# Attention of the two later layers: heads alternating per query block, and value products per query block in 128 columns

## What is computed

```python
for l in range(2):
    h = rmsnorm(x)
    p = h @ w_in[l]                       # latents of queries and keys, a shared rope key, a convolution's input
    q, k, v = ...                         # 8 heads: queries and keys of 64 + 32 rotated columns, values of 64
    sc = q @ k.T                          # per head 512 x 512
    prob = softmax(sc * scale)            # over all 512 keys, no mask
    y_attn = prob @ v                     # per head 512 x 64
    u = silu(layernorm(dwconv(glu(p))))   # depthwise convolution of 31 taps
    x = x + concat(y_attn, u) @ w_o[l]
    x = x + ffn(rmsnorm(x))
```

## Time and profile before

| | |
|---|---|
| runs, median | 2052.92 us |
| profiled execution, its span | 2052.9 us (no time lies around the span) |
| PE, DVE, ACT busy | 1956.8, 1195.2, 958.2 us |
| chain that ended last | PE 88%, DVE 6%, ACT 3% |
| attention loop, first later layer | 887.4 to 988.4 us |
| attention loop, second later layer | 1516 to 1617 us |

### The profile page before, as it was taken

One profiled execution on the slowest core, in us unless ns is written; L12 is line 12 of the kernel. 1 busy time (PEld: TensorE's weight loads), 2 busy tenths in 40 slices (PEclk: granted clock), 3 DMA queues, 4 the chain that ended last, 5 costly groups with the idle time before them and its releaser, 6 DMA issues.

```text
span 2052.9 us, 25795 instructions
## 1 busy us (share of the span) xinstructions
PE 1956.8 (95%) x8419; PEld 1542.7 (75%) x8419; DVE 1195.2 (58%) x1960; ACT 958.2 (47%) x1722; POOL 146.7 (7%) x148
## 2 busy tenths in 40 slices
PE   8999989699999989999999999999999999999997
PEld 6777778578878867765678887887765678888786
DVE  4554456633333346888576665536688657666534
ACT  4665663333433333477553443434377644334432
POOL 2111000200000003220010000003120010000000
PEclk9999999899999998999999999999999999999999
DMA  4222213133323322211123333233221033333332
GB/s 136 62 62 72 67 54 101 41 101 95 96 93 97 97 72 63 64 35 35 49 80 108 92 100 100 92 97 83 67 42 42 21 100 87 102 97 92 96 94 81
DMA packets 163423, 162.44 MB, mean 79 GB/s; under 512 B 46840, under 2 KB 121550, under 8 KB 163340
## 3 DMA queue, kind: packets, MB, share of 16 engines
q1 hardware_dynamic: 163236, 161.36, 27.0%
q10 hardware_dynamic: 104, 0.03, 0.0%
HBM read 159.24 MB, written 2.10 MB: 79 GB/s over the span
## 4 chain that ended last, share of the span: by engine, by line
PE 88%; DVE 6%; ACT 3%; issue 1%; POOL 1%; DMA 0%; SPq 0%; DVEq 0%; ACTq 0%; POOLq 0%
PE bank_b L2066 15%; PE bank_b L2068 14%; PE bank_b L2067 14%; PE bank_a L2066 12%; PE bank_a L2068 12%; PE bank_a L2067 12%; PE bank_b L2357 3%; PE bank_b L2455 2%; PE bank_a L2168 1%; PE bank_a L2441 1%; DVE arena L1343 1%; DVE x_t L1340 1%; DVE w_lo L1340 1%; DVE arena L1340 1%; DVE h_lo L1343 1%
## 5 line engine op out<-in xcount | busy, mean ns | idle before, releaser
L1340 DVE TENSOR_TENSOR w_lo<-w_raw,w_hi 128x512 fp32r<-128x512 f32 (+3 forms) x621 | 427.9, 701 | 622.1 <-ACT w_hi L1054 374.3
L1054 ACT ACTIVATE w_hi<-w_raw 128x512 fp32r<-128x512 f32 (+3 forms) x396 | 233.1, 599 | 451.0 <-PE bank_b L2068 233.9
L2066 PE MATMUL bank_b<-h_hi,w_hi 128*128 128x512 f32 x944 | 371.2, 393 | 7.4 <-DVE var L1358 3.9
L2067 PE MATMUL bank_b<-h_lo,w_hi 128*128 128x512 f32 x944 | 367.8, 390 | 0.0
L2068 PE MATMUL bank_b<-h_hi,w_lo 128*128 128x512 f32 x944 | 367.8, 390 | 0.0
L2066 PE MATMUL bank_a<-h_hi,w_hi 128*128 128x512 f32 x592 | 236.3, 399 | 30.4 <-DVE h_lo L1343 16.3
L771 ACT ACTIVATE w_hi<-w_raw 128x512 fp32r<-128x512 f32 x225 | 137.8, 629 | 261.8 <-PE bank_b L2068 140.6
L1343 DVE SCALAR_TENSOR_TENSOR arena<-arena,cols_all 128x512 f32<-128x512 f32 x350 | 245.2, 753 | 0.1
L2067 PE MATMUL bank_a<-h_lo,w_hi 128*128 128x512 f32 x592 | 233.9, 395 | 0.0
L2068 PE MATMUL bank_a<-h_hi,w_lo 128*128 128x512 f32 x592 | 233.5, 394 | 0.0
L2066 PEld LDWEIGHTS bank_b<-h_hi,w_hi 128*128 128x128 f32 x944 | 177.5, 188 | 48.9 <-issue 4.9
(11 more groups left out here) (262 smaller groups left out, 2496.8 us busy)
## 6 DMA issues: line engine op xcount, KB each, us to landing
w_raw<-in_w_up_dram SPq DMA_DIRECT2D x240, 256.0 KB, 3.1
w_raw<-in_w_down_dram SPq DMA_DIRECT2D x152, 256.0 KB, 2.6
w_raw<-in_w_in_dram SPq DMA_DIRECT2D x64, 128.0 KB, 2.4
w_raw<-in_w_gate_dram SPq DMA_DIRECT2D x32, 256.0 KB, 2.9
w_raw<-in_w_in_dram SPq DMA_DIRECT2D x32, 256.0 KB, 2.7
w_raw<-in_w_o_dram SPq DMA_DIRECT2D x32, 256.0 KB, 2.6
w_raw<-in_w_out_dram SPq DMA_DIRECT2D x16, 256.0 KB, 2.7
w_raw<-in_w_in_dram SPq DMA_DIRECT2D x16, 192.0 KB, 2.4
```

The costliest lines, as they stand in the source:

```text
L1054: nc.scalar.activation(w_hi[:, s, 0:c], w_raw[:, s, 0:c], ACT.Copy).then_inc(w_round, 1)
L1340: return nc.vector.tensor_tensor(out_, a, b, op)
L2066: nc.tensor.matmul(out_, a_hi, b_hi, start=start, stop=False, skip_group_check=loose)
L2067: nc.tensor.matmul(out_, a_hi, b_lo, start=False, stop=False, skip_group_check=loose)
```

## The change

The heads of a pair now alternate: block g is query block g // 2 % 4 of head g % 2. `values2(j)` runs in every second step, the odd ones from step 7 on, and makes one query block's output for both heads of the pair: two heads by four key blocks, eight products of 128 moving columns each, with the same stationary tiles of `vv` with their zero columns. `PV_LAG` is 6 where it was 8. `pts` is a ring of eight blocks, each copied whole. `round_out(i - 1)` stands in step m = 6 where `round_out(i - 2)` stood in m = 0, and the remainder that DVE takes from it in m = 7 where it was m = 1. The first values of pair 1, and so the wait for `conv_base`, are in step 15. The loop is two steps shorter.

```diff
--- before.py
+++ after.py
@@ -62,7 +62,7 @@
 DVE_TAPS = CONV_K - PE_TAPS
 HALO = CONV_K // 2
 BLOCKS = PAIRS * 2 * TT
-EXP_LAG, TURN_LAG, PV_LAG = 2, 4, 8
+EXP_LAG, TURN_LAG, PV_LAG = 2, 4, 6
 CONV_STEPS = ({}, {}, {0: 2, 1: 2, 5: 2, 6: 2}, {8: 2, 9: 2, 13: 2, 14: 2})
 FF2 = 2816
 F2T = FF2 // P
@@ -159,7 +159,7 @@
-    "vv_zero": (0, 1), "pv_done": (0, 2 * PAIRS), "tap_done": (0, HT * DVE_TAPS), "diag_made": (0, HT * PE_TAPS),
+    "vv_zero": (0, 1), "pv_done": (0, PAIRS * TT), "tap_done": (0, HT * DVE_TAPS), "diag_made": (0, HT * PE_TAPS),
@@ -329,7 +329,7 @@
 
         un = arena[:, 0:4, :]
         lat_hi, lat_lo = split[:, 0:5, :], split[:, 5:10, :]
-        pts = (arena[:, 0:4, :], sq[:, :, :])
+        pts = [arena[:, n, :] for n in range(4)] + [sq[:, n, :] for n in range(4)]
 
         kq_hi, kq_lo = ([[h[:, 2 * q + hd, :] for hd in range(2)] for q in range(2)] for h in (h_hi, h_lo))
         kk_hi, kk_lo = ([[h[:, 4 + 2 * q + hd, :] for hd in range(2)] for q in range(2)] for h in (h_hi, h_lo))
@@ -1182,7 +1182,7 @@
 
                 def round_out(i):
 
-                    act.wait_ge(pv_done, was[pv_done.name] + 2 * i + 2)
+                    act.wait_ge(pv_done, was[pv_done.name] + (i + 1) * TT)
                     nc.scalar.activation(o2_hi[:, i, :], bank_b[:, i % 2, :], ACT.Copy).then_inc(o_round, 1)
 
                 for g in range(BLOCKS + TURN_LAG + 1):
@@ -1199,14 +1199,11 @@
                     n = g - TURN_LAG
                     if 0 <= n < BLOCKS:
 
-                        b, head = n % TT, n // TT
                         act.wait_ge(pt_made, was[pt_made.name] + n + 1)
-                        if b == 0 and head >= 2:
-
-                            act.wait_ge(pv_done, was[pv_done.name] + head - 1)
-                        nc.scalar.activation(pts[head % 2][:, :, b * P:b * P + P],
-                                             bank_a[:, n % 2, :].rearrange("p (k q) -> p k q", k=TT),
-                                             ACT.Copy).then_inc(pt_ready, 1)
+                        if n >= len(pts):
+
+                            act.wait_ge(pv_done, was[pv_done.name] + (n - len(pts)) // 2 + 1)
+                        nc.scalar.activation(pts[n % len(pts)], bank_a[:, n % 2, :], ACT.Copy).then_inc(pt_ready, 1)
                     n = g - EXP_LAG - 1
                     if 0 <= n < BLOCKS:
 
@@ -1231,8 +1228,8 @@
                             stage_q(i + 1, 1)
                         if m in (1, 3, 4, 5):
                             split2(M_PAIR + (i + 2) * SLOTS + (1, 3, 4, 5).index(m))
-                    if m == 0 and i >= 2:
-                        round_out(i - 2)
+                    if m == 6 and i >= 1:
+                        round_out(i - 1)
                 round_out(PAIRS - 1)
                 split2(M_WO + 4)
                 for j in range(HT):
@@ -1935,9 +1932,9 @@
                             stage_q_lo(i + 1, 1)
                         if m in (2, 4, 5, 6):
                             split2_lo(M_PAIR + (i + 2) * SLOTS + (2, 4, 5, 6).index(m))
-                    if m == 1 and 2 <= i:
-                        dve.wait_ge(o_round, was[o_round.name] + i - 1)
-                        rest(o2_lo[:, i - 2, :], bank_b[:, i % 2, :], o2_hi[:, i - 2, :]).then_inc(o_split, 1)
+                    if m == 7 and 1 <= i:
+                        dve.wait_ge(o_round, was[o_round.name] + i)
+                        rest(o2_lo[:, i - 1, :], bank_b[:, (i - 1) % 2, :], o2_hi[:, i - 1, :]).then_inc(o_split, 1)
                     taps(taps_by(g, first_taps) - tap)
                 dve.wait_ge(o_round, was[o_round.name] + HT)
                 rest(o2_lo[:, 3, :], bank_b[:, 1, :], o2_hi[:, 3, :]).then_inc(o_split, 1)
@@ -2417,7 +2414,7 @@
 
                 def scores2(g):
 
-                    i, hd, b = g // (2 * TT), g // TT % 2, g % TT
+                    i, b, hd = g // (2 * TT), g // 2 % TT, g % 2
                     c = slice(b * P, b * P + P)
                     if b == 0:
                         pe.wait_ge(qk_ready, was[qk_ready.name] + i * 4 + 3 + hd)
@@ -2431,31 +2428,35 @@
 
                 def transposed(g):
 
-                    b = g % TT
                     if g >= 2:
 
                         pe.wait_ge(pt_ready, was[pt_ready.name] + g - 1)
                     pe.wait_ge(p_ready, was[p_ready.name] + g + 1)
                     for kb in range(TT):
                         c = slice(kb * P, kb * P + P)
-                        last = nc.tensor.transpose(bank_a[:, g % 2, c], prob[:, b, c], ident[:, :])
+                        last = nc.tensor.transpose(bank_a[:, g % 2, c], prob[:, g % TT, c], ident[:, :])
                     last.then_inc(pt_made, 1)
 
-                def values2(n):
-
-                    i, hd, kb = n // (2 * TT), n // TT % 2, n % TT
-                    if kb == 0:
-                        pe.wait_ge(pt_ready, was[pt_ready.name] + n + TT)
-                        if hd == 0 and i == 0:
-                            pe.wait_ge(vv_ready, was[vv_ready.name] + TT)
-                            pe.wait_ge(vv_zero, was[vv_zero.name] + 1)
-                        if hd == 0 and i >= 2:
-
-                            pe.wait_ge(o_split, was[o_split.name] + i - 1)
-                    part = nc.tensor.matmul(bank_b[:, i % 2, :], vv[:, kb, i, hd * P:hd * P + P], pts[hd][:, kb, :],
-                                            start=hd == 0 and kb == 0, stop=hd == 1 and kb == TT - 1)
-                    if kb == TT - 1:
-                        part.then_inc(pv_done, 1)
+                def values2(j):
+
+                    i, b = j // TT, j % TT
+                    c = slice(b * P, b * P + P)
+                    pe.wait_ge(pt_ready, was[pt_ready.name] + 2 * j + 2)
+                    if j == 0:
+                        pe.wait_ge(vv_ready, was[vv_ready.name] + TT)
+                        pe.wait_ge(vv_zero, was[vv_zero.name] + 1)
+                    if j == TT:
+
+                        pe.wait_ge(conv_base, was[conv_base.name] + HT)
+                    if b == 0 and i >= 2:
+
+                        pe.wait_ge(o_split, was[o_split.name] + i - 1)
+                    for hd in range(2):
+                        for kb in range(TT):
+                            last = nc.tensor.matmul(bank_b[:, i % 2, c], vv[:, kb, i, hd * P:hd * P + P],
+                                                    pts[(2 * j + hd) % len(pts)][:, kb * P:kb * P + P],
+                                                    start=hd == 0 and kb == 0, stop=hd == 1 and kb == TT - 1)
+                    last.then_inc(pv_done, 1)
 
                 def beside(i, m):
 
@@ -2481,11 +2482,8 @@
                     if 0 <= g - TURN_LAG < BLOCKS:
                         transposed(g - TURN_LAG)
                     beside(i, m)
-                    if g >= PV_LAG:
-                        if g - PV_LAG == 2 * TT:
-
-                            pe.wait_ge(conv_base, was[conv_base.name] + HT)
-                        values2(g - PV_LAG)
+                    if g >= PV_LAG and (g - PV_LAG) % 2:
+                        values2((g - PV_LAG) // 2)
                     for j in range(HT):
                         if g in CONV_STEPS[j]:
                             if j == 3 and done[j] == 0:
```

## The result

The kernel after took 2067.95 us, the median of 4 runs (2066.74 to 2069.14); the kernel before, run beside it, 2052.86 (4 runs, 2052.21 to 2054.88). The ratio is 1.0069, with a 95% interval of 1.0057 to 1.0081, so it is slower by 15.1 us where 11 were forecast. The profiled execution took 2069.03 us, its span 2067.3.

A forecast was written before the change was run, and what follows sets the result against it. PE was taken to bound the kernel, busy 1956.8 of 2052.9 us. Terms +2.3 + 1.3 + 0.3 + 2.5 + 0 - 0.8 made +5.6 per layer, +11.2 for two: 2064 us, range 2056 to 2070 for 8 in 10.

The forecast's parts named there:

- Price of the products: Value products in both later layers: 0.11 us per 128-column matmul, 28.2 us per layer where 27.5 stood.
- the dear products: Rival on the value products: 0.19 us per small matmul, +20 us per layer, 2101 us in all; chance 0.04.
- the rule as the prediction took it: Value products: full-height weight loads do not overlap, so a half product takes 0.21 us and the term is +27 per layer.
- Steps 7 to 15: Early attention-loop steps, as long as PE works: five value blocks replace eight products, +2.3 us per layer.
- The new wait in step 15: PE waits for base(3) on ACT before its values in step 15: 1.3 us per layer, bounds 0 and 2.0.
- Steps 16 to 25: Loop steps whose end DVE sets; PE's imbalance is mostly absorbed by existing waits: +0.3 us per layer.
- paid by waits that were there: Steps 16 to 25: the 0.85 us of step 16 and waits of steps 22 and 24 fall into existing waits.
- Steps 26 to 31: Last pair: even steps last 2.01 us, odd ones 2.97, 14.9 where 12.43 stood, +2.5 per layer.
- nothing measurable: Rival: even steps last 1.16 us, only the price of the products is left, some 2053 us (2050 to 2057); chance 0.11.
- Steps 32 to 34, and the end: Steps without scores unchanged from 6.27 us; after the last turn 3.96 us instead of 4.76, -0.8 per layer.
- The span "with nothing around it": Whole kernel: the profiled span of 2052.9 us was taken to equal the median of the runs.
- The rival "faster": Steps 17 to 25: DVE's heavy steps meet PE's long ones, a layer gains 3.5 us, giving 2046; chance 0.04.

The follow-up runs named there:

- e1_even8: Kernel after with values spread evenly, one head's four small products in every step, PV_LAG 8, round_out in m = 0: 2055.78 us, ratio 1.0012.
- e5_after_base: Kernel after with base(3) moved on ACT from step 15 to step 14, ahead of the exponential of step 15: 2063.69 us, ratio 1.0046.
- e4_after_fill: Kernel after with eight unused 512-column products behind the scores of step 24, in the wait ahead of step 25: 2064.08 us, ratio 1.0047.
- e3_before_odd: Kernel before with its 512-column value products placed two by two in odd steps, none in even ones: 2060.24 us, ratio 1.003.
- the second comparison: Both kernels unchanged, timed side by side once more: after 2066.25 us, before 2055.06, ratio 1.0062.
- e2_odd8: Kernel after with PV_LAG back to 8 and round_out in m = 0, values still all eight in odd steps: 2062.16 us, ratio 1.004.
- e8_mid: e7_tail with the values of steps 18 to 20 moved into steps 21 to 24: 2042.54 us, ratio 0.9939.
- e7_tail: e1_even8 with values from behind the loop packed in: two half blocks in each of steps 32 to 34, one in 35 and 36: 2051.41 us, ratio 0.9987.

## Why the prediction was right, point by point

- **Price of the products: right.** 0.106 us per small matmul (0.11 forecast). The trace of after, and e1_even8 with +0.5 us per layer, rule out the dear products. The Trainium skill ("TensorE: Matmul & The Clock Gate", The mechanism) lets a weight load overlap only when it is for another row group, though the same section also has loads for a background weight buffer pulled ahead. Here each of the sixteen matmuls has its own load of 0.19 us over the whole height, and they follow each other 0.106 apart: the measurement decides against the rule as the prediction took it.
- **Steps 7 to 15: right.** 34.18 us from 904.81 to 938.99, where before had 30.92: +3.26, against 2.3 + 1.3 forecast. Without the 1.26 that e5_after_base takes off step 15 it is +2.0. The prediction's own terms give 2.2 (8.8 + 0.3 less 6.9), not 2.3.
- **The new wait in step 15: right.** 1.3 was forecast. PE's idle time there is 1.02, but by the starts the wait is 1.19, and e5_after_base, which moves `base(3)` alone, shortens step 15 by 1.26 and the loop by 1.3: all of it is on the path.
- **Steps 16 to 25: the one step that failed in its size.** +0.3 was forecast, +1.50 measured. The mechanism that I gave holds: from the turn of step 16, step 21 starts on DVE at 14.6 (14.8 forecast), takes 3.79, steps 22 and 23 take 6.82 (6.8), and the turn of step 25 comes 1.66 behind step 24's maximum (1.65). That is +0.07. What I left out is that a longer wait of PE ahead of step 25 can come with a fall of its clock: 1.43 us. I said of PE's imbalance there that it was "paid by waits that were there"; in time it was, in clock not. At full clock, in e4_after_fill and e5_after_base, step 25 lasts 2.94 or 2.95 and these 1.4 to 1.6 us are gone.
- **Steps 26 to 31: right.** 14.81 us (970.27 to 985.08) where 12.43 were, +2.38 (+2.5 forecast). Even steps last 1.99 and not 1.16, with 0.69 or 0.70 idle before each odd one, which rules out the rival "nothing measurable". e3_before_odd shows that the lump alone makes steps of 1.99 and 2.88, and e1_even8 that the same small products without lumps give 2.03 to 2.06.
- **Steps 32 to 34, and the end: right.** 6.22 where 6.27 were; 4.27 where 5.09 were to the second `w_o` product, so -0.8 as forecast. To the first `w_o` product it is 3.96 (4.0 forecast) and was 4.46 (983.67 to 988.13), not 4.8: behind a 512-column float32 product the next record starts early, and its successor follows 0.63 later, which is why the second one is taken.
- **The sum.** The terms measured are 3.26 + 0.07 + 2.38 - 0.05 - 0.82 = 4.84 per layer without the clock. e4_after_fill, at full clock, has +4.81 and +4.90, 9.7 for both, against the 11.2 forecast. The fall of the clock adds 1.5 and 1.6 (kernel after less e4_after_fill). The loops' 12.8 and the medians' 15.1 differ by 2.3 us; that part did not repeat (the second comparison gave 2066.25 less 2055.06 = 11.2), and falls of the clock outside the loops are of this size (+2.8 and -1.6 in the two profiles). By experiments, a layer's +4.8 is: lumps +3.15 (e2_odd8 less e1_even8), small products and alternating heads +0.5 (e1_even8), shorter distance with its wait +1.2 (e4_after_fill less e2_odd8). That the medians of the second comparison differ by just the 11.2 that were forecast is in part luck: the terms that I had were 1.5 us too large for the two layers, and the fall of the clock that I had left out adds 3.1.
- **The span "with nothing around it": wrong.** Where both are given, an execution lies 1.7 us above its span, in both kernels (2069.03 and 2067.3; 2054.13 and 2052.4). It is the same for both, so the difference is untouched.
- **The rival "faster"** had its place right: DVE does set steps 21 to 24. It needed the opposite of this change, which lightens steps 22 and 24. e8_mid put the work into those steps and gained 2.6 us per layer over e7_tail, which has the same work elsewhere.

Open: why the clock falls at a wait of 1.93 in the kernel after and not at 1.94 in e5_after_base, and in one loop of two in e3_before_odd. The length of the wait alone does not decide it. Open too is how the half us of e1_even8 divides between small products and alternating heads; no run changes one alone.

## What to carry to other kernels

Small work that stands in every step of a loop over two engines is filler, and it costs next to nothing as long as each step stays at the loop's floor (2.02 us against 2.01 here); lumping it into every second step pays in the full steps and got almost nothing back in the empty ones. Before moving such work, list each step's idle time and put the work where the step waits for another engine, as e8_mid does. And look at the clock of the window behind each wait that a change makes longer.

## What the runs showed of the hardware

- Plain float32 products of 128 columns with a new weight load each run at a quarter of the 512-column ones: 0.106 us per matmul against 0.43. Four products of 128 columns and the rounded 512-column product behind them take 1.13 us (e1_even8), one product of 512 columns and the same product behind it 1.09 (before).
- At the end of waits of 1.8 to 2.8 us, or just behind them, PE's granted clock was at times 0.50, and back at 1.00 after some 3 us (step 25) to 7 us (at 1413 us in the kernel after). The same wait of the same kernel (2.79 us) showed it in one execution and not in the next; others (1.93, and 2.2 in the kernel before) showed it both times. Such falls outside the loops moved whole spans by 1.6 to 2.8 us.
- Eight products that nobody needs, put into a wait of PE, cost nothing, and the loops with them were 1.5 us shorter at a clock of 1.00. That they kept the clock up is not shown, since it stayed up in five of six loops with such a wait left empty.
